# Splitting every second weight transfer of nine projections, with the low halves on VectorE, and three moved pieces of work

## What is computed

```
h = rms_norm(x, norm_g)
proj = jnp.einsum('bsd,de->bse', h, w_in)
u_lru, u_s5, qkv_ret, q_nsa, kv_nsa, bg_nsa, gate_paths, merge = split_columns(proj, IN_SIZES)
y_lru, y_s5, y_ret, y_nsa = ...
ys = ys * jax.nn.silu(gate_paths.reshape(bsz, s, N_BRANCH, BRANCH_W))
branch = jnp.einsum('bsnw,nwd->bsnd', ys, w_branch)
merged = jnp.sum(jax.nn.sigmoid(merge.reshape(bsz, s, N_BRANCH, d)) * branch, axis=2)
return x + jnp.einsum('bsd,de->bse', merged, w_out)
```

## Time and profile before

| | |
|---|---|
| median of 3 runs | 884.82 us (884.59 to 884.88) |
| the profiled execution | 886.77 us |
| its span, first to last instruction | 885.0 us |
| mean granted TensorE clock | 0.976 |
| PE busy | 838.8 us, 95% of the span |
| DVE, ACT, POOL busy | 421.6, 378.4, 303.7 us |
| HBM read | 124.85 MB, 142 GB/s over the span |

### The profile page before, as it was taken

How to read it: one execution, slowest core, us unless ns; L and a number is a source line. 1 busy time by engine, 2 the same in 40 slices (tenths; PEclk the granted TensorE clock), 3 DMA queues, 4 the chain that set the end, 5 groups by cost and what they waited for, 6 DMA issues and landing times.

```text
span 885.0 us, 10537 instructions
## 1 busy us (share of the span) xinstructions
PE 838.8 (95%) x4094; PEld 639.0 (72%) x4094; DVE 421.6 (48%) x689; ACT 378.4 (43%) x709; POOL 303.7 (34%) x135
## 2 busy tenths in 40 slices
PE   6889999999979799999989999999998997999997
PEld 5776678444868688888878757854477786888885
DVE  2847131116389662533676524101717965535325
ACT  2454444001745345554436527410056434554542
POOL 3000000001667756667500000000056676666760
PEclk8979999999999989999999999999999998999999
DMA  7326354544453443435444562554462443445441
GB/s 228 79 73 235 113 172 138 161 148 144 168 163 117 134 131 124 138 127 181 142 90 131 172 196 73 192 155 152 142 214 95 121 142 118 143 143 167 152 158 47
DMA packets 86993, 126.58 MB, mean 143 GB/s; under 512 B 22072, under 2 KB 32672, under 8 KB 86944
## 3 DMA queue, kind: packets, MB, share of 16 engines
q1 hardware_dynamic: 86768, 125.88, 45.3%
q10 hardware_dynamic: 176, 0.04, 0.0%
HBM read 124.85 MB, written 1.05 MB: 142 GB/s over the span
## 4 chain that ended last, share of the span: by engine, by line
PE 79%; DVE 8%; ACT 5%; issue 4%; POOL 2%; DMA 1%; SPq 0%; POOLq 0%; DVEq 0%; ACTq 0%
PE proj L1623 29%; PE proj L1666 22%; PE proj L1662 11%; PE M L1618 3%; POOL w_lo L675 2%; PE M L1757 2%; PE M L1784 2%; ACT sc L697 2%; ACT nkT L697 1%; PE M L1937 1%; PE M L558 1%; PE M L1942 1%; DVE sc L1500 1%; PE M L1907 1%; PE proj L1692 1%
## 5 line engine op out<-in xcount | busy, mean ns | idle before, releaser
L675 POOL TENSOR_TENSOR w_lo<-raw,w_hi 128x1024 fp32r<-128x1024 f32 x112 | 285.6, 2578 | 526.9 <-ACT w_hi L697 495.6
L1666 PE MATMUL proj<-raw,h_full 128*128 128x512 f32 (+1 forms) x512 | 210.1, 568 | 0.0
L1666 PEld LDWEIGHTS proj<-raw,h_full 128*128 128x128 f32 x512 | 96.3, 190 | 104.2 <-issue 101.4
L697 ACT ACTIVATE w_hi<-raw 128x1024 fp32r<-128x1024 f32 x120 | 122.7, 1050 | 65.4 <-PE proj L1623 28.1
L1623 PE MATMUL proj<-w_hi,h_hi 128*128 128x512 f32 x320 | 128.4, 401 | 0.5 <-POOL w_lo L675 0.5
L1623 PE MATMUL proj<-w_lo,h_hi 128*128 128x512 f32 x320 | 125.0, 390 | 0.0
L1623 PE MATMUL proj<-w_hi,h_lo 128*128 128x512 f32 x320 | 124.9, 390 | 0.0
L1662 PE MATMUL proj<-h_full,raw 128*128 128x256 f32 x512 | 116.3, 387 | 0.0
L1662 PEld LDWEIGHTS proj<-h_full,raw 128*128 128x128 f32 x512 | 97.9, 194 | 15.3 <-issue 2.0
L1623 PEld LDWEIGHTS proj<-w_hi,h_hi 128*128 128x128 f32 x320 | 60.1, 188 | 13.8 <-issue 1.1
L1623 PEld LDWEIGHTS proj<-w_hi,h_lo 128*128 128x128 f32 x320 | 60.1, 188 | 13.1
(11 more groups left out here) (324 smaller groups left out, 1150.7 us busy)
## 6 DMA issues: line engine op xcount, KB each, us to landing
raw<-in_w_in SPq DMA_DIRECT2D x152, 512.0 KB, 3.5
raw<-in_w_branch SPq DMA_DIRECT2D x32, 512.0 KB, 3.5
raw<-in_w_out SPq DMA_DIRECT2D x16, 512.0 KB, 3.5
raw<-in_s_w_glu SPq DMA_DIRECT2D x8, 512.0 KB, 3.6
raw<-in_w_in SPq DMA_DIRECT2D x8, 256.0 KB, 2.5
merged<-in_nsa_ck_w SPq DMA_DIRECT2D x4, 512.0 KB, 5.5
mt<-in_nsa_ck_w SPq DMA_DIRECT2D x4, 512.0 KB, 7.7
merged<-in_nsa_cv_w SPq DMA_DIRECT2D x4, 512.0 KB, 5.4
```

What stands on the lines that cost most here:

```text
L675: nc.gpsimd.tensor_tensor(w_lo[:, slot(s, l), 0:n * w], raw[:, u % N_RAW, 0:n * w], w_hi[:, slot(s, l), 0:n * w].bitcast(f32), ALU.subtrac ...
L697: i = nc.scalar.activation(out_, in_, func, **kw)
L1666: last = mm(ps[:, 512 * t:512 * t + w], h_full[:, k, t * P:(t + 1) * P], rw, start=st_, stop=sp_, skip_group_check=True)
```

## The change

- Of nine chunks of the first half (ret_v, nsa_kv, gate_s5, gate_lru, merge_s5_0, merge_s5_1, ret_q, ret_k, nsa_q) the second and fourth unit become split units, with the low half on VectorE; the first and third stay native. These are units 13, 15, 17, ..., 47. u_s5, cmp and u_lru stay wholly native.
- So h_hi and h_lo are made early: h_hi on ScalarE before `spread_w(0)`, h_lo on VectorE behind `make_v(1)`.
- GpSimd clears s5x, gate and sc at once, ahead of the two inverse roots, where it was behind them.
- TensorE turns S5's weights later: `turn_w(0, 0)` behind the first half of cmp, `turn_w(0, 1)` behind the second, and `state_inputs(0)` behind the first half of u_lru. ScalarE's `keep_wT` and others are moved to suit.
- VectorE's `scan` is cut into three parts with low halves between them, and the convolution of RG-LRU (`conv`) stands behind `skip(0)` instead of ahead of `rope_ret(1)`.
- The compressed scores' two halves stand together on TensorE, ahead of a unit of merge_lru_1 and a group of transposes.

```diff
-NATIVE = ("u_s5", "cmp", "u_lru", "ret_v", "nsa_kv", "gate_s5", "gate_lru", "merge_s5_0", "merge_s5_1", "ret_q", "ret_k", "nsa_q")
-SPLIT_UNITS = [u for u in range(NU) if CHUNKS[UNITS[u][0]][0] not in NATIVE]
-LO_ON_VECTOR = ("out_0b", "out_1b")
+NATIVE = ("u_s5", "cmp", "u_lru")
+HALF_NATIVE = ("ret_v", "nsa_kv", "gate_s5", "gate_lru", "merge_s5_0", "merge_s5_1", "ret_q", "ret_k", "nsa_q")
+def is_split(u):
+    name = CHUNKS[UNITS[u][0]][0]
+    return name not in NATIVE and not (name in HALF_NATIVE and UNITS[u][1] in (0, 4))
+SPLIT_UNITS = [u for u in range(NU) if is_split(u)]
+LO_ON_VECTOR = ("ret_v", "nsa_kv", "gate_s5", "gate_lru", "merge_s5_0", "merge_s5_1", "ret_q", "ret_k", "nsa_q",
+                "out_0b", "out_1b")
...
@@ gpsimd
+                        pool.memset(s5x[:, 2048:4096], 0.0).then_inc(cleared, 1)
+                        zero_blocks(pool)
                         for t in range(TT):
                             inverse_root(pool, 0, t)
-                        zero_blocks(pool)
-                        pool.memset(s5x[:, 2048:4096], 0.0).then_inc(cleared, 1)
...
@@ scalar
-                    next_cast("cmp")
+                    act.wait_ge(chunk_done, ch("cmp"))
...
+                    cast_units(UNIT_END[CHUNK["u_lru"]] + 1)
                     act.wait_ge(cmpT_done, 1)
...
-                    keep_ms(0)
-                    spread_w(1)
                     next_cast("u_lru")
                     run(u_lru[:, :, 3:T + 3], pr("u_lru")[:, :].rearrange("p (t n) -> p t n", t=KB), ACT.Copy, evac("u_lru"))
+                    cast_units(UNIT_END[CHUNK["ret_v"]] + 1)
+                    spread_w(1)
+                    keep_ms(0)
                     keep_wT(1, 0)
                     next_cast("ret_v")
...
+                    keep_wT(1, 1)
                     trig(1)
-                    keep_wT(1, 1)
+                    cast_units(UNIT_END[CHUNK["nsa_kv"]] + 2)
+                    spread_v(1)
                     keep_y(0)
-                    spread_v(1)
...
                     merge_chunk("s5", 0)
                     act.wait_ge(hid_arg, 1)
                     run(hid_q, hid_q, ACT.Tanh, hid_tanh, scale=GELU_C)
-                    merge_chunk("s5", 1)
-                    cast_units(UNIT_END[CHUNK["ret_q"]] + N_SPLIT)
+                    cast_units(UNIT_END[CHUNK["merge_s5_1"]] + 2)
                     act.wait_ge(z_arg, 1)
                     run(gelu_t, gelu_t, ACT.Tanh, z_tanh, scale=GELU_C)
+                    merge_chunk("s5", 1)
...
@@ vector
-                    scan(0)
+                    split_lo("ret_v", 1)
+                    scan_in(0)
+                    scan_steps(0)
+                    split_lo("ret_v", 3)
+                    scan_out(0)
                     angles(1)
-                    scan(1)
+                    split_lo("nsa_kv", 1, 3)
+                    scan_in(1)
+                    split_lo("gate_s5", 1)
+                    scan_steps(1)
+                    scan_out(1)
+                    split_lo("gate_s5", 3)
                     skip(0)
+                    conv()
+                    split_lo("gate_lru", 1, 3)
                     skip(1)
...
+                    split_lo("merge_s5_0", 1, 3)
                     dve.wait_ge(hid_tanh, 1)
...
                     v.tensor_tensor(gelu_t, gelu_t, yf, ALU.mult).then_inc(z_arg, 1)
-                    rope_ret(0, "ret_q")
+                    split_lo("merge_s5_1", 1, 3)
                     dve.wait_ge(z_tanh, 1)
...
@@ tensor
                     turn_c()
-                    turn_w(0, 0)
                     chunk("cmp", 0)
+                    turn_w(0, 0)
+                    chunk("cmp", 1)
                     turn_w(0, 1)
-                    chunk("cmp", 1)
+                    chunk("u_lru", 0)
                     state_inputs(0)
-                    chunk("u_lru", 0)
...
                     compressed_scores(0)
+                    compressed_scores(1)
                     chunk("merge_lru_1", range(1, 2))
                     pe.wait_ge(yg_ready, 3)
                     blocks_T(1024, flat(gate[:, 0])).then_inc(rnT_done, 1)
-                    compressed_scores(1)
                     chunk("merge_lru_1", 1)
```

More of the change, by code:

```diff
@@ L839, in keep_y @@
                                     ACT.Copy, y_ready if i == LC - 1 and d == 3 else None)
+                    act.wait_ge(hfull_done, KD)
+                    for k in range(0, KD, 2):
+                        run(flat(h_hi[:, k:k + 2, :]), flat(h_full[:, k:k + 2, :]), ACT.Copy, hhi_done)
                     spread_w(0)
@@ L847, in _ @@
                     keep_u(1)
-                    keep_wT(0, 1)
+                    keep_wT(0, 0)
                     keep_u(2)
@@ L943, in _ @@
                     gate_chunk("s5")
-                    act.wait_ge(hfull_done, KD)
-                    for k in range(0, KD, 2):
-                        run(flat(h_hi[:, k:k + 2, :]), flat(h_full[:, k:k + 2, :]), ACT.Copy, hhi_done)
                     keep_y(1)
@@ L1194, in scan, with scan_steps @@
                         dve.wait_ge(bu_used, h + 1)
+                    def scan_steps(h):
+                        t0, t1, t2, t3 = (s5_t[:, f] for f in range(4))
                         v.tensor_tensor(t0, t0, t1, ALU.add)
@@ L1198, in scan, with scan_out @@
                         link(v.tensor_tensor_scan(flat(t3), flat(ang_a), flat(t2), 0.0, ALU.mult, ALU.add))
+                    def scan_out(h):
+                        cos, sin = cos_sin[:, 0], cos_sin[:, 1]
+                        t0, t1, t2, t3 = (s5_t[:, f] for f in range(4))
                         if h:
@@ L1280, in branch, with tap, conv @@
                             v.tensor_tensor(dst, dst, m, ALU.add).then_inc(mt_free, 1)
+                    def tap(k, t):
+                        return vec[:, V_CONV + KB * k + t:V_CONV + KB * k + t + 1]
+                    def conv():
+                        dve.wait_ge(evac("u_lru"), ev("u_lru"))
+                        for t in range(KB):
+                            i = v.tensor_scalar(xc[:, t, :], u_lru[:, t, 0:T], tap(0, t), vec[:, V_CONVB + t:V_CONVB + t + 1],
+                                                ALU.mult, ALU.add)
+                        link(i)
+                        for k in range(1, 4):
+                            for t in range(KB):
+                                i = v.scalar_tensor_tensor(xc[:, t, :], u_lru[:, t, k:k + T], tap(k, t), xc[:, t, :], ALU.mult, ALU.add)
+                            if k < 3:
+                                link(i)
+                        i.then_inc(xc_ready, 1)
                     dve.wait_ge(v0_ready, 1)
@@ L1284, in _ @@
                     make_v(1)
+                    for k in range(0, KD, 2):
+                        dve.wait_ge(hhi_done, k // 2 + 1)
+                        v.tensor_tensor(flat(h_lo[:, k:k + 2, :]), flat(h_full[:, k:k + 2, :]),
+                                        flat(h_hi[:, k:k + 2, :]).bitcast(f32), ALU.subtract).then_inc(hlo_done, 2)
                     e, s_, s2, q_, m_ = S(1)[:, 0:4], S(6)[:, 0:4], S(6)[:, 4:8], S(7)[:, 0:4], S(7)[:, 4:8]
@@ L1361, in _ @@
                     v.tensor_tensor(yf, yf, gelu_t, ALU.mult).then_inc(z_ready, 1)
+                    split_lo("ret_q", 1)
                     dve.wait_ge(z_hi, 1)
                     v.tensor_tensor(flat(ys_lo[:, :, :]), yf, flat(ys_hi[:, :, :]).bitcast(f32), ALU.subtract).then_inc(z_lo, 1)
[L1366 to L1380 removed]
+                    split_lo("ret_q", 3)
+                    split_lo("ret_k", 1, 3)
+                    rope_ret(0, "ret_q")
+                    split_lo("nsa_q", 1, 3)
                     rope_ret(1, "ret_k")
@@ L1640, in chunk @@
                             _, k0, nk, _ = UNITS[u]
-                            if name in NATIVE:
+                            if u not in SPLIT_UNITS:
                                 pe.wait_ge(raw_loaded[u % N_RAW], raw_target[u])
@@ L1667, in chunk @@
                                                       start=st_, stop=sp_, skip_group_check=True)
-                                elif kind == "u":
+                                elif name in ("gate_s5", "gate_lru"):
                                     for m in range(4):
@@ L1802, in _ @@
                     last.then_inc(cmpT_done, 1)
+                    chunk("u_lru", 1)
                     chunk_kernels(0)
-                    chunk("u_lru", 1)
+                    pe.wait_ge(hlo_done, KD)
                     chunk("ret_v", 0)
```

29 lines of the change are left out of this document (6 added, 23 removed).

## The result

The changed kernel takes 890.23 us (median of 12 runs, 886.81 to 891.68), the kernel before beside it 885.0 us (median of 12). The ratio is 1.0054, with a 95% interval of 1.0042 to 1.0067: slower by half a per cent. The forecast was 890.6 us. The experiments' groups had the kernel before beside them too, at medians of 884.9 to 885.5 us, so that runs of different groups can be compared to about half a microsecond. Of the profiled execution the span is 887.7 us, against 885.0 before; the one execution took 0.7 us less than its kernel's median, the other 1.8 us more.

The account below looks back on a forecast made before the run. TensorE, in use for 95% of the span, was taken to bound the kernel. Terms -6.9 - 24.4 - 1.6 + 11.0 + 13.2 + 4.0 + 13.2 - 0.7 - 2.0 gave +5.8 us, so 890.6 us, range 873 to 900.

Parts of the forecast that it names:

- the start: Kernel's beginning: early memsets ready VectorE's first identity sooner and keep turn_x's clock high; -6.9 us (0 to -7.7).
- A: Before turn_w(1, 0), both layers: TensorE waits 5.5 us as ScalarE casts unit 15 first; +11.0 us (0 to 12).
- B: Before unit 33, both layers: TensorE waits 6.6 us, hid_tanh standing behind unit 35's cast; +13.2 us (11 to 14).
- C: At gate_s5's PSUM, both layers: store of nsa_kv behind unit 23's cast; 2.0 us each, +4.0 us (0 to 6).
- the products: TensorE, both layers: split units save 19.0 us in seven chunks and 5.4 in eight gate units; -24.4 us.
- S5's turns: Layer 0, new order: wait ends at the same time, clock fall costs less; -1.6 us (-5.0 to +1.0).
- the scores: Compressed scores: ScalarE's exp stays behind qT<-M, so TensorE's 4.55 us wait shrinks by 0.35; -0.7 us.
- the second half: Each layer's second half: glu's units issued together bring ScalarE's lru work forward; -2.0 us.
- the clock: Behind A and B, both layers: TensorE's granted clock falls, 3.3 us for each of four; +13.2 us (7 to 20).
- rival 1: Clock stays high over A and B, both layers: 877.4 us, chance 0.18.
- Unit 15 didn't land early: Rival claimed unit 15's load lands after 3.6 us, A shrinking to 1.0 us without its falls: 875.0 us, chance 0.09.
- rival 4: Compressed scores pay in full, 3.5 us more a layer and a fall avoided: 877.0 us, chance 0.05.

Follow-up runs that it names:

- the start alone: Kernel before, with only GpSimd's three memsets moved ahead of the inverse roots: 878.98 us, ratio to before 0.9935.
- A, B and C mended: Changed kernel with unit 15's cast and low half later, hid_tanh earlier, unit 23's cast behind the store of nsa_kv: 850.25 us.
- the run where GpSimd was idle: Changed kernel with ScalarE's exp of the compressed scores ahead of the copy qT<-M: 875.39 us.
- only A's first half mended: Changed kernel with unit 15 cast behind ScalarE's store of u_lru, spread_w(1) and keep_ms(0): 882.93 us.

## Why the prediction was right

**The sum.** +5.8 us forecast, +5.2 measured between the medians. The range of 873 to 900 us held it near its middle, and slower had the larger chance. The runs price the parts. The kernel before with the start alone takes 878.98 us and the one with A, B and C mended 850.25: between them lie the products, S5's turns, the scores and the second half, 28.7 us. The prediction had 24.4 + 1.6 + 0.7 + 2.0 = 28.7. How these share it is seen for the products only (0.70 us a unit instead of 0.68), and to the tenth the agreement is luck. So the large terms, some 35 us gained and 40 lost, are both right; below them some errors cancel, as the paragraph on the clock shows.

**The start.** -6.9 us forecast, 6.4 and 5.9 measured. VectorE begins the identities at 9.71 us and takes 0.48 us for both, and turn_x ran at full clock, as said: u_s5 begins at 13.73 instead of 20.88 us. In the kernel before with the early memsets turn_x ran at 0.66, and u_s5 begins at 15.36.

**The three waits.** A 5.5 us forecast, 5.49 and 4.30 in the trace; B 6.6, and 6.48 and 6.19; C 2.0, and 2.50 and 2.29. 28.2 us together, 27.3 found. Releasers, casts and landings are those named: the landings took 8.3, 4.7 and 4.6 us, with 8.1, 5.0 and 5.0 counted. Counting each queue from one start to the instruction that TensorE wants was enough for this.

**The clock.** It fell behind A and B in both layers, so rival 1 (0.18) didn't come. 3.3 us a fall was the term with the largest miss: in the traces the four cost 8.9 us, 2.2 each, with 13.2 forecast. The price lay between one fall of 5.0 us, where state_inputs(0)'s small matmuls followed, and one of 1.8; dense work behind a wait is nearer to the lower one. At u_s5 too 3.4 us were put and 1.6 measured; but the old order's fall, counted at 5.0 from the kernel before, is 3.3 in the changed kernel, so that their difference came out as forecast. A, B and C with their clock cost 40.0 us by the mends, with 11.0 + 13.2 + 4.0 + 13.2 = 41.4 forecast. That is near because two errors cancel: the falls were put 4 us too high, and about as much went elsewhere, in small steps that no term held, most of them in the second halves of the layers. What they are stays open. The estimate by the Trainium skill's 1%, 8.9 us, is the cost of these four by chance: it was meant for all falls, which come to some 18.

**Rivals.** Unit 15 didn't land early (8.3 us). The start did give. The scores did not pay in full: 8.4 us of waits remained of 9.1. Yet rival 4 named the price that ScalarE's order kept back: 13.6 us forecast for it, 14.8 measured once the exp was moved (8.4 of waits and some 6 of clock, where 7.0 and 6.6 were put).

**What the prediction didn't see.** That behind A stands a second wait by VectorE's order (2.1 us), hidden as long as A lasts, and that the slow products of the scores are a matter of when GpSimd works.

## What to carry to other kernels

A cast or any other instruction that waits for a load, put into an engine's queue ahead of small work that another engine needs, hands the load's delay on to that engine (here 12.6 us on ScalarE, 5.5 of them on TensorE): before such a change is written off as slower, list for each queue what stands behind each load-dependent instruction. Here the change gave some 29 us by its products, its other new places and the second half, and 6 by its start, and three of its new places took 40 away; their reordering, without one computing instruction more or less, turned +0.5% into -4.0%, and one more, of the scores' exp, gave most of the step to -5.6%. When a wait is removed, look at once for the next one that it hid, on the engine between, as A's second half on VectorE.

## What the hardware showed

- VectorE's two small products at the compressed scores took 1.98 us and 2 x 2.41 while GpSimd formed low halves, and 0.17 and 2 x 0.29 in the run where GpSimd was idle. The slow ones end at 300.57, 303.00 and 305.35 us, each just behind the end of a low half of GpSimd (300.54, 302.85, 305.20). The Trainium skill (SBUF — State Buffer, SBUF: two separate sides) says that a VectorE instruction with two SBUF inputs and a GpSimd instruction that reads SBUF shut each other out for the length of a whole instruction; the trace agrees by these times; the low halves last 2.4 us here.
- ScalarE's copy of every fourth float32 of a row took 374 ns out of PSUM and 661 ns out of SBUF. In the same stretch of the changed kernel copies of 256 elements in runs of 16 or more took 374 ns out of PSUM (sc<-M) and 410 ns out of SBUF (sc<-sc), so the step costs about 250 ns out of SBUF and nothing out of PSUM. The Trainium skill (Advanced Engine Details and Errata, SBUF Cachelines) has a penalty where each access falls into another 16-byte line, without a number; the trace agrees.
- 86 matmuls whose results nobody reads made the kernel 8.5 us faster, by keeping the granted clock at 1.00 behind four waits. A fall of the clock cost 1.8 to 2.6 us where dense products followed.
- With equal waits of 0.85 us, turn_x ran at a clock of 1.00 in one kernel's execution and at 0.66 in another's; behind C's waits of 2.3 to 2.6 us the clock was 1.00 in one execution and 0.57 to 0.65 in another. In the run with only A's first half mended ten executions spread over 9.3 us, against 4.9 of the changed kernel's twelve.
